# A seven-product input projection, in windows of column pairs and three token passes, in place of the direct one

## The reference

```python
h = _rmsnorm(x, norm_g) * (1 + scale[:, None]) + shift[:, None]
z = h @ w_in
q, k, v, gate_a, r_f, r_b, u, gate_b, mg_a, mg_b = jnp.split(z, idx, axis=-1)
q = _apply_rope(q, rope[0], rope[1])
k = _apply_rope(k, rope[0], rope[1])
g_f = jax.nn.log_sigmoid(r_f @ w_af + b_af) / GATE_NORM
...
y_a = (_rmsnorm(o, gla_norm_g).reshape(B, T, GLA_VDIM) * jax.nn.silu(gate_a)) @ w_proj_a
merged = jax.nn.sigmoid(mg_a) * y_a + jax.nn.sigmoid(mg_b) * y_b
x = x + gate[:, None] * (merged @ w_out)
```

## Time and profile before

| | us |
|---|---|
| median of 3 runs | 2268.07 |
| lowest and highest | 2262.85, 2270.06 |
| span of the profiled execution | 2259.7 |
| last matmul of its projection | 1340.1 |
| its attention, Fourier mix and output projections | 1352 to 2259.7 |

### The profile page before, as it was taken

One profiled execution on the slowest core, in us unless ns is written; L12 is line 12 of the kernel. 1 busy time (PEld: TensorE's weight loads), 2 busy tenths in 40 slices (PEclk: granted clock), 3 DMA queues, 4 the chain that ended last, 5 costly groups with the idle time before them and its releaser, 6 DMA issues.

```text
span 2259.7 us, 33049 instructions
## 1 busy us (share of the span) xinstructions
PE 2129.4 (94%) x12121; PEld 1845.1 (82%) x12121; DVE 721.1 (32%) x1255; ACT 613.5 (27%) x1384; POOL 451.4 (20%) x340
## 2 busy tenths in 40 slices
PE   7699999999999999999999989998957999998998
PEld 2488889999888888888888867776857999997886
DVE  2867771000010001001001005557687222223423
ACT  2646661111111111111111116766523011012221
POOL 1500000000433223142322310004242111111212
PEclk9899999999999999999999989999978999999999
DMA  7334442212545445454544557554133343454443
GB/s 299 115 109 155 152 158 75 83 61 83 176 150 186 150 159 174 159 173 154 182 153 155 170 171 312 215 205 165 47 149 124 113 125 116 121 189 153 132 147 112
DMA packets 178437, 340.70 MB, mean 151 GB/s; under 512 B 14610, under 2 KB 120268, under 8 KB 173360
## 3 DMA queue, kind: packets, MB, share of 16 engines
q1 hardware_dynamic: 178352, 339.64, 43.2%
HBM read 215.84 MB, written 123.74 MB: 150 GB/s over the span
## 4 chain that ended last, share of the span: by engine, by line
PE 79%; issue 7%; DVE 6%; DMA 3%; ACT 3%; POOL 1%; SPq 0%; POOLq 0%; ACTq 0%; DVEq 0%
PE bank L1409 44%; PE bank L1613 15%; PE bank L1470 9%; PE bank L1498 3%; PE bank L1517 1%; PE bank L1519 1%; PE bank L1518 1%; PE bank L1505 1%; DMA x_in<-in_x 1%; ACT junk L770 1%; DVE zb L384 1%; POOL yt L750 1%; DVE uf L1267 1%; DVE h L1023 1%; PE bank L1526 1%
## 5 line engine op out<-in xcount | busy, mean ns | idle before, releaser
L1409 PE MATMUL bank<-h_hi,w_hi 128*128 128x512 f32 (+1 forms) x1640 | 606.3, 370 | 6.7 <-POOL h_lo L691 5.6
L1409 PE MATMUL bank<-h_lo,w_hi 128*128 128x512 f32 (+1 forms) x1640 | 605.4, 369 | 0.0
L1409 PE MATMUL bank<-h_hi,w_lo 128*128 128x512 f32 (+1 forms) x1640 | 604.4, 369 | 0.0
L1409 PEld LDWEIGHTS bank<-h_hi,w_hi 128*128 128x128 f32 x1640 | 310.2, 189 | 59.6 <-issue 5.8
L1409 PEld LDWEIGHTS bank<-h_hi,w_lo 128*128 128x128 f32 x1640 | 309.9, 189 | 52.5
L1409 PEld LDWEIGHTS bank<-h_lo,w_hi 128*128 128x128 f32 x1640 | 310.3, 189 | 51.5
L1057 DVE CAST w_hi<-w_raw 128x1024 fp32r<-128x1024 f32 x48 | 36.6, 762 | 870.2 <-PE bank L1409 672.8
L845 ACT ACTIVATE stage<-bank 128x512 f32<-128x512 f32 (+1 forms) x160 | 88.7, 555 | 682.0 <-PE bank L1409 682.0
L1613 PE MATMUL bank<-in_hi,pw_hi 128*128 128x256 f32 x864 | 245.9, 285 | 12.2 <-DVE in_lo L1292 12.2
L1613 PE MATMUL bank<-in_lo,pw_hi 128*128 128x256 f32 x864 | 245.6, 284 | 0.0
L1613 PE MATMUL bank<-in_hi,pw_lo 128*128 128x256 f32 x864 | 245.6, 284 | 0.0
(11 more groups left out here) (178 smaller groups left out, 2876.1 us busy)
## 6 DMA issues: line engine op xcount, KB each, us to landing
w_raw<-in_w_in SPq DMA_DIRECT2D x49, 512.0 KB, 3.9
dec_in<-e_dram SPq DMA_DIRECT2D x48, 384.0 KB, 3.5
rope<-in_rope SPq DMA_DIRECT2D x48, 384.0 KB, 4.1
qk_dec<-dec_in SPq DMA_DIRECT2D x48, 384.0 KB, 2.9
mg_ld<-mg_dram SPq DMA_DIRECT2D x72, 256.0 KB, 2.9
e_dram<-decs SPq DMA_DIRECT2D x32, 512.0 KB, 3.0
mg_dram<-stage SPq DMA_DIRECT2D x64, 256.0 KB, 2.0
wada<-in_w_ada SPq DMA_DIRECT2D x6, 2048.0 KB, 8.1
```

Of the source, the lines that this page charges most:

```text
L1409: ins = pe.matmul(bank[out][:, 0:n], w[0][:, k, sl], h[:, k, t0:t0 + n], start=(k == 0 and w is w_hi and h is h_hi), stop=(k == KT - 1 and ...
```

## The change

The 48 column tiles outside the ranks are taken in 24 pairs (`PAIRS`), and the tokens in three passes of 768, each as two blocks of 384. One pair in one pass is a window; there are 72 windows. The 2 x 2 blocks of a window (two halves of the model width, two column tiles, two token blocks) are multiplied with seven block products in place of eight, in Winograd's form: sums and differences of input blocks (h32, s1, s2) and of weight blocks (w_raw, w_sum) are formed first, each of the seven operands is split into high and low, and the four result quarters come out of sums of the products. The order of the operations is again written out.

```diff
+NP = 3
+BW = 384
+PAIRS = ([("qk", 0), ("u", 0), ("v", 0), ("qk", 1), ("u", 1), ("v", 1), ("qk", 2), ("v", 2), ("ga", 0), ("qk", 3), ("v", 3)]
+         + [("ga", i) for i in range(1, 4)] + [("gb", i) for i in range(2)] + [("mg", i) for i in range(8)])
+NPROD = 7
+RING = 8
+GATE_WINDOWS = (1, 2, 4, 5, 7, 8, 10, 11)
+X_WINDOWS = tuple(range(14, 14 + TP))
```

On GpSimd, the weight sums of the window after the next:

```diff
+            def sum_weights(n, which):
+                t1, t2, t4 = (w_sum[:, k, :, :] for k in range(3))
...
+                    if n:
+                        pool.wait_ge(s_wlo, NPROD * (n - 1) + 4)
+                    pool.tensor_tensor(t1, b12, b11, ALU.subtract).then_inc(s_t, 1)
```

ScalarE's loop over the windows (`high_weights` splits off high parts, `use` makes the logs of a gate block, or takes transposes out of PSUM):

```diff
+            for p in range(NP):
+                waiting = []
+                for w in range(NW):
...
+                    if n:
+                        other_quarters(n - 1)
+                    high_weights(n + 1, 0)
+                    for i in waiting:
+                        decays(p, i)
+                    waiting = []
+                    if w in GATE_WINDOWS:
+                        act.preload_act_table_set("natural_log_exp_and_others")
...
+                    for j in range(NPROD):
+                        if j == 0:
+                            copy_first(n)
+                        elif j == 2:
+                            first_quarter(n)
+                        if j == 3:
+                            for i in waiting:
+                                decays(p, i)
+                            waiting = []
+                        for u in uses[j]:
+                            use(p, w, u)
...
+                        if j:
+                            high_weights(n + 1, j)
```

VectorE's queue inside the same two loops:

```diff
+                    add_product(n, 0)
+                    low_weights(n + 1, 1)
...
+                    low_weights(n + 1, 2)
+                    if gates:
+                        gate_sums(p, gates[0])
...
+                    add_product(n, 1)
+                    low_weights(n + 1, 3)
...
+                    add_product(n, 2)
+                    low_weights(n + 1, 4)
+                    if gates:
+                        gate_sums(p, gates[1])
```

TensorE's product j of a window, with what it waits for:

```diff
-            def unit_block(slot, b, a, out):
...
+            def product(p, w, j):
...
+                if j == 0 and n >= 2:
+                    pe.wait_ge(s_c11, n - 1)
+                elif j == 1 and n >= 2:
+                    pe.wait_ge(s_d, 5 * (n - 2) + 4)
+                elif j == 2:
+                    pe.wait_ge(s_p1, n + 1)
+                elif j == 3:
+                    pe.wait_ge(s_d, 5 * n + 1)
+                elif j == 4 and n >= 2:
+                    pe.wait_ge(s_d, 5 * (n - 2) + 5)
+                elif j == 5:
+                    pe.wait_ge(s_d, 5 * n + 2)
+                elif j == 6:
+                    pe.wait_ge(s_d, 5 * n + 3)
+                first = j in (0, 1, 4)
+                for k in range(HK):
+                    for wt, h in ((w_hi, h_hi), (w_hi, h_lo), (w_lo, h_hi)):
+                        ins = pe.matmul(bnk[:, 0:BW], wt[slot][:, k, :], h[:, j, k, :],
```

More of the change, by code:

```diff
@@ new lines, in build, with out_tile, stores_of, stored_before @@
+        W_SUMS = (0, 3, 0, 1, 2, 0, 4)
+        def out_tile(n):
+            p, w, kind, i = pair(n)
+            if kind == "qk":
+                return qk_s[i % 2][:, :, :].rearrange("p c (b t) -> p c b t", b=2)
+            return outs[n % 2][:, :, :, :]
+        def stores_of(n):
+            kind = PAIRS[n % NW][0]
+            return {"qk": 0, "v": 2}.get(kind, 1)
+        def stored_before(n):
+            return sum(stores_of(m) for m in range(n % 2, n, 2))
+        def quads_done(n):
+            return 5 * n + 5
@@ new lines, in gate_unit, with window_uses @@
+        def gate_unit(i):
+            return i // 4, i // 2 % 2, i % 2
+        def window_uses(p, w):
+            uses = {j: [] for j in range(NPROD)}
+            if w == 0:
+                uses[6] += [("rank", 0), ("rank", 1)]
+            if w in GATE_WINDOWS:
+                i = 2 * GATE_WINDOWS.index(w)
+                uses[0].append(("gate", i))
+                uses[3].append(("gate", i + 1))
+            if w and PAIRS[w - 1][0] == "v":
+                for j, q in ((1, (0, 0)), (2, (1, 1)), (4, (1, 0)), (5, (0, 1))):
+                    uses[j].append(("v", q))
+            if p + 1 < NP and w in X_WINDOWS:
+                uses[3].append(("x", 0))
+                uses[5].append(("x", 1))
+            if p + 1 == NP and w in ADA_WINDOWS:
+                uses[3].append(("ada", ADA_WINDOWS.index(w)))
+            return uses
@@ L1473, in _ @@
[L1473 to L1481 removed]
+            for e in range(6, 2 * KT):
+                turn_x0(e)
+            pe.wait_ge(s_mod, 2)
+            pe.wait_ge(s_ha0, KT)
@@ L1483, in pe_head @@
+            for p in range(NP):
+                for w in range(NW):
+                    uses = window_uses(p, w)
+                    for j in range(NPROD):
+                        product(p, w, j)
+                        for u in uses[j]:
+                            use(p, w, u)
+            pe.wait_ge(s_c11, LAST + 1)
+            pe.wait_ge(s_d, quads_done(LAST))
+            pe.wait_ge(s_gc, len(use_number))
             def pe_head(head, n, i):
```

1180 lines of the change are left out of this document (643 added, 537 removed).

## The result

The changed kernel takes 2514.2 us (median of 4, 2512.3 to 2516.8); the kernel before took 2267.9 beside it. The ratio is 1.109, 95% interval 1.107 to 1.110. The change makes the kernel 11% slower. The forecast, 2288 us with a range to 2355, missed by 226 us. The profiled execution spans 2511.4 us.

A forecast was written before the change was run, and what follows sets the result against it. TensorE, busy 94% of the span, bounds the kernel. First window 100, work 1099, gate losses 130, rest 28 make 1357 against 1340.1; with 3 at the end, +20: 2288 us, 0.9% slower, range 2205 to 2355.

The forecast's parts named there:

- TensorE's work: Projection: 0.1735 us per 384-column matmul, 14.57 us a window; 1099 us without a wait for all windows but the first.
- Rival 3: Products slower than 0.1735 us a matmul because weight loads hide less well behind 384 columns; given no share.
- GpSimd slows it: Gate windows: VectorE's SBUF operations slow beside GpSimd; losses over three passes 167 us disturbed against 90 free.
- I take 130, midway: Gate-window loss over three passes set between 167 us disturbed and 90 free, since GpSimd idles while waiting for VectorE.
- The undisturbed base: Gate windows without GpSimd's slowing: 30 us lost a pass, 90 in three passes.
- SiLU's share: Third and fourth heads' gate windows: table loads and SiLU lengthen waits; undisturbed, a head loses 10.5 us against 4.4.
- all late stores, rank lows and input windows: Late stores, rank low parts and input windows of the projection together: 12 us.
- The chain in the queues: Gate windows: products 5 and 6 wait for VectorE's additions, product 2 of the next for ScalarE; 2.2 us each window undisturbed.
- The start: First window: modulation 5 us later than 47.5, inputs at 58, window ends near 100; 88 unslowed, 106 if copies queue.
- The windows between passes: Between passes: ScalarE's high parts, table loads and the last pair's sigmoid lose 8 us each, 16 for two.
- Rival 2: TensorE's clock falls to 0.50 for 3.2 us behind long waits: up to 38 us more, 2363 us; chance 0.17.
- Rival 1: Waits are hidden, gate windows lose under 1 us each: 2167 us; chance 0.21 including what lies between.

The follow-up runs named there:

- Run 5: GpSimd's q/k head operations (turn, decay products) and its weight sums narrowed to 8 columns of each block, waits kept, in the changed kernel: 2367.4 us.
- run 9: In the changed kernel, six windows a pass have VectorE's gate scans read and write their running sums in PSUM, nothing left out: 2473.5 us.
- run 10: In the changed kernel, windows 8 and 11 of each pass take a rectifier in place of SiLU, so no SiLU table loads there: 2470.9 us.
- run 1: In the changed kernel, SyncE's queue puts the v pair's store ahead of the half swaps and the decayed q/k store: 2503.7 us.
- run 3: In the changed kernel, ScalarE's decays moved later: second block's behind the next window's product 0 copy, first block's one product later: 2482.8 us.
- run 6: In the changed kernel, gate logs, scans and differences of heads 1 to 3 narrowed to 8 columns of a block, waits kept: 2457.9 us.
- Run 11: In the changed kernel, start-up reordered: rank and gate weights copied later, product 0's copy and first addition earlier, nothing left out: 2501.3 us.
- Run 7: In the changed kernel, filler matmuls into an unread bank keep TensorE busy in its longest waits, at eight places a pass: 2511.9 us.
- runs 13 to 16: GpSimd work moved to VectorE. Changed kernel: 13 weight sums 2536.7 us, 16 turn and decay 2508.2. With reorderings and late SiLU: 14 sums 2392.6, 15 both 2410.5.

## Why the prediction was wrong

**TensorE's work** was right: 0.1738 us a matmul, and merge windows of 14.6 us. Rival 3 had no share and gets none. One small term was short: the two ada rows, 6.9 in the sum, lengthen windows 16 and 17 of the last pass by (21.9 - 14.6) + (21.8 - 14.6) = 14.5.

**The step that failed is "GpSimd slows it", and with it "I take 130, midway".** The earlier trace rows has operations of equal length side by side; I read them as both slowed in proportion and gave the whole effect 77 us, of which I took 40. What stands in its place: a VectorE operation whose operands all lie in SBUF stands still until GpSimd's is over. The lengths in those rows couldn't tell the two apart; operations of unequal length do (1.58 us for three columns, 3.94 for a low part). The ends could have: VectorE's operation of the earlier trace rows from 1685.55 ends at 1687.29, 0.55 us behind the end of this one of GpSimd, the same distance as in the changed kernel.

```profile
1685.04 1.70 POOL L393 TENSOR_TENSOR sb<-zb 128x512 f32<-128x512 f32 x1
```

Run 5 puts the price of all of GpSimd's work at 146.8 us, 132 of it in the head windows, and run 9 shows the condition. That "GpSimd is idle while it waits for VectorE" was the reason for midway, and it was no relief: GpSimd's two longest waits for VectorE's low parts come to 530 us in the changed kernel, and the price in the head windows was still 132 us, not 77, of which the forecast took 40.

**The undisturbed base was too low as well**, 158 us against 90 in the head windows of run 5. SiLU's share of it was about right, 37 us for 43.3 in run 10, though that run was made beside GpSimd. Missing was the wait for the v store in windows 4 and 7, 57.2 us of ScalarE's time in the changed kernel and 58.0 in run 5. I had put all late stores, rank lows and input windows at 12. The issue of the store alone (run 1) gave only 10.5 us, so how much of the 68 is the store and how much the order behind it stays open; with ScalarE's order, sums in PSUM and the start together it is part of 113.7.

**The chain in the queues was right in kind.** Products 5 and 6 wait for VectorE's additions and product 2 for ScalarE's copy, as foretold, and runs 3, 6 and 9 shorten just that. Its timing was not: I let the turn start at 3.6 us in the window, behind a swap transfer scaled from the earlier trace rows. In window 8 it starts at 803.27 - 795.99 = 7.3, on top of the scans and the subtraction. DMA issues of the page, KB and us to landing:

```profile
swap<-qk_s SPq DMA_DIRECT2D x48, 192.0 KB, 6.7
v_dram<-outs SPq DMA_DIRECT2D x24, 384.0 KB, 7.1
```

**The start** was 26 us short: it was to end "near 100", or at "106 if the copies queue too". They did queue, behind the rank and gate weights, which the forecast didn't have in ScalarE's queue ahead of product 0. Run 11 gives back 13. The other half was there earlier. The forecast had the modulation ready 5 us later than 47.5, an estimate that no row bore out; it is ready at 65.1, 12.6 later still:

```profile
37.52 2.82 PE L1591 MATMUL bank<-consts,x_a 128*128 128x128 f32 x12 [17.15 <-DVE x_d L1192]
...
41.56 21.03 PE L1581 MATMUL bank<-wada,silc 128*2 128x512 f32 x48
...
64.96 0.17 DVE L1279 TENSOR_TENSOR modu<-modu,cols 128x16 f32<-128x16 f32 x1
```

Transposes of x stand in TensorE's queue ahead of 48 of the ada matmuls and wait 17.15 us for VectorE; that is the likeliest reason, and no run moves them.

**The windows between passes** took 14 us of loss each, not 8, and the input windows 2.6 to 2.7 over 14.6, of which 0.9 is their transposes (48 x 0.118 / 6); the rest goes with a wait of some 1.5 for ScalarE's copy. No run was made for these 39 us alone.

**Rival 2, the clock,** looked true: mean 0.92, and by the distances between their starts 627 matmuls of the projection ran at 0.31 us, 83 us more than at full rate. Run 7 takes 20 us of that away and gains nothing measurable. In its window 9 the slow matmuls were free, behind a wait that VectorE sets; that the other 63 us were free too is argued and not shown. **Rival 1**, hidden waits, was to decide from gate losses under 110 us; they were 290, and it is out.

## What to carry to other kernels

Count the time of GpSimd's operations with tensors in SBUF as time in which VectorE's SBUF operations may stand still, and add it to VectorE's own, window by window, before calling either engine free. It is an upper bound: GpSimd was busy for 711 us up to the last product, and run 5 took 504 of these away and 266 of VectorE's. Where a queue chain is tight, give VectorE's operations an operand in PSUM (40.7 us here), or remove GpSimd's work; moving that work to VectorE did not pay here (runs 13 to 16). When several queues wait for each other, single repairs show less than they are worth: 95.6 us apart, 113.7 together.

## What was not expected of the hardware

- An operation on 8 columns beside GpSimd takes 646 ns in the mean and a copy of 3 columns 1.58 us in one case: the stall lasts until GpSimd's operation ends, whatever the length of one's own.
- A scan with one input and its output in PSUM takes 408 ns in a kernel whose SBUF scans take 1242, and 406 when it starts inside an operation of GpSimd.
- Raising TensorE's granted clock in one window from 0.89 to 1.00 changed its length by nothing, 15.37 us both times.
- The transfer of 192 KB that swaps the halves took 6.7 us to land, where 96 KB had taken 2.4.
